# The first weight piece of a stage, loaded by the stage before it into a lasting tile, and small products placed behind two groups of the projections

## The reference, cut to what matters

```python
# first block, layer 0 (RWKV mixer, then a gated feed-forward), layer 1 (gated delta rule, feed-forward)
lerp = lambda i: u + xx * mu[i]
w_log = -softplus(-(w0 + tanh(lerp(3) @ w1) @ w2)) - 0.5      # w1: D x 64, w2: 64 x D
a = sigmoid(a0 + (lerp(4) @ a1) @ a2)                          # a1: D x 64, a2: 64 x D
...
proj = u @ w_in                                                # gated delta rule: D x (4 D + 16)
...
x = layer_norm(ALPHA * x + (1 + ga1) * (y @ w_out), ...)       # every mixer ends like this
gate, up = split(u @ ffn_w_in[i], 2)                           # D x 2*2816
x = layer_norm(ALPHA * x + (1 + ga2) * ((silu(gate) * up) @ ffn_w_out[i]), ...)
# second block: a state-space mixer (x @ w_in, D x 5152), mixture of experts, dilated attention, experts
```

## Time and profile before

| what | value |
|---|---|
| median of 3 runs | 4761.02 us (4743.81 to 4763.74) |
| the profiled execution's own time | 4764.29 us |
| its span, first to last instruction | 4762.6 us |
| PE busy | 3911.8 us, 82% of the span |
| VectorE, ScalarE, GpSimd busy | 34%, 15%, 15% |
| mean granted clock of PE | 0.904 of full speed |
| largest waits of PE | experts for their weights 127.8 us in 48, experts for VectorE 67.1 us in 66 |

### The profile page before, as it was taken

The page is one execution under the profiler, slowest core; times in us unless marked ns, Lnnn a source line. Parts: engine busy times, 40 slices in busy tenths (PEclk is TensorE's granted clock), DMA queues, the critical chain, the costliest instruction groups (busy, mean ns, idle before and its releaser), DMA issues. The chain is left out here.

```text
span 4762.6 us, 56977 instructions
## 1 busy us (share of the span) xinstructions
PE 3911.8 (82%) x23207; PEld 2625.4 (55%) x23207; DVE 1642.3 (34%) x3018; ACT 706.3 (15%) x1502; POOL 719.7 (15%) x595
## 2 busy tenths in 40 slices
PE   4989978999898878999899895877749977577773
PEld 2578855784446756864458743444427755344442
DVE  6667735530365653211341512000031143300003
ACT  2211211010222222100211500000010122000000
POOL 1123303330110213420100101000010033100001
PEclk9999978999899988999899896998969977699987
DMA  3221313623121012221221026999932100599995
GB/s 124 64 80 53 111 49 133 212 98 110 39 68 36 2 50 80 84 89 53 67 77 36 1 80 244 392 396 397 393 127 71 53 1 27 232 396 397 399 396 225
DMA packets 242989, 707.37 MB, mean 149 GB/s; under 512 B 22140, under 2 KB 117828, under 8 KB 192100
## 3 DMA queue, kind: packets, MB, share of 16 engines
q1 hardware_dynamic: 223060, 660.99, 37.5%
q10 hardware_dynamic: 15120, 26.76, 1.6%
q0 software_dynamic: 4608, 16.78, 0.9%
HBM read 667.24 MB, written 37.24 MB: 148 GB/s over the span
## 5 line engine op out<-in xcount | busy, mean ns | idle before, releaser
L3037 PE MATMUL experts_pg<-moe_wg,experts_xt 128*64 128x256 f32 x4224 | 529.4, 414 | 142.3 <-DMA moe_wg<-in_moe_w_up 127.8
L3037 PEld LDWEIGHTS experts_pg<-moe_wg,experts_xt 128*64 128x64 f32 x4224 | 334.5, 150 | 320.2 <-issue 178.0
L465 PE MATMUL ffn_out_y<-ffn_out_ring,ffn_h 128*128 128x512 f32 x704 | 308.8, 601 | 20.8 <-DMA ffn_out_ring<-in_ffn_w_out 20.8
L3052 PE MATMUL experts_py<-moe_wd,experts_ht 128*64 128x512 f32 x1056 | 256.4, 629 | 41.6 <-DVE experts_ht L3104 24.2
L86 PE MATMUL att_proj_ps<-att_proj_ring,ut 128*128 128x512 f32 x576 | 250.0, 597 | 15.6 <-DMA att_proj_ring<-in_attn_w_qkv 15.6
L3102 DVE TENSOR_TENSOR experts_h<-experts_hs,experts_pg 128x256 f32<-128x256 f32 x66 | 27.8, 421 | 659.2 <-ACT experts_hs L3071 659.2
L465 PEld LDWEIGHTS ffn_out_y<-ffn_out_ring,ffn_h 128*128 128x128 f32 x704 | 135.3, 193 | 190.5 <-issue 169.0
L562 PE MATMUL ffn_in_seven<-ffn_in_seven_t,ffn_in_seven_s 128*128 128x256 f32 x1056 | 238.4, 383 | 0.0
L86 PEld LDWEIGHTS att_proj_ps<-att_proj_ring,ut 128*128 128x128 f32 x576 | 177.5, 308 | 87.8 <-DMA att_proj_ring<-in_attn_w_qkv 16.0
L562 PEld LDWEIGHTS ffn_in_seven<-ffn_in_seven_t,ffn_in_seven_s 128*128 128x128 f32 x1056 | 204.0, 193 | 29.1
L562 PE MATMUL ffn_in_seven<-ut,ffn_in_ring 128*128 128x256 f32 x704 | 181.8, 404 | 19.1 <-DMA ffn_in_ring<-in_ffn_w_in 19.1
(11 more groups left out here) (651 smaller groups left out, 6294.0 us busy)
## 6 DMA issues: line engine op xcount, KB each, us to landing
moe_wg<-in_moe_w_gate SPq DMA_DIRECT2D x66, 2048.0 KB, 20.6
moe_wg<-in_moe_w_up SPq DMA_DIRECT2D x66, 2048.0 KB, 25.2
moe_wd<-in_moe_w_down SPq DMA_DIRECT2D x66, 2048.0 KB, 26.2
ffn_in_ring<-in_ffn_w_in SPq DMA_DIRECT2D x44, 1024.0 KB, 5.8
ffn_in_ada_ring<-in_ada_w SPq DMA_DIRECT2D x28, 1024.0 KB, 7.6
ffn_out_ring<-in_ffn_w_out SPq DMA_DIRECT2D x22, 1024.0 KB, 5.0
ssd_proj_ring<-in_ssd_w_in SPq DMA_DIRECT2D x20, 1024.0 KB, 5.3
att_proj_ring<-in_attn_w_qkv SPq DMA_DIRECT2D x9, 2048.0 KB, 7.9
```

Of the source, the lines that this page charges most:

```text
L465: last = nc.tensor.matmul(y[:, tt, half, :], h[:, kk, tt * P:(tt + 1) * P], ring[:, n % RING, q, half * BANK:(half + 1) * BANK], start=(kk ...
L3037: last = nc.tensor.matmul(pg[ch * SLOTS:(ch + 1) * SLOTS, b, side, 0:HH], xt[:, b, kk % MQ, kk // MQ, :], wg[:, b, side, kk, ch * HH:(ch + ...
L3052: last = nc.tensor.matmul(py[half * SLOTS:(half + 1) * SLOTS, b, :], ht[:, b, kk % HM, kk // HM, :], wd[:, b, kk, half * HALF:(half + 1) * ...
```

## The change

A tile `ahead` of 8 KB per partition and a semaphore live as long as the program does. Class `Ahead` holds a list of nine first pieces in the order of use; `next` issues the DMA of the next one. `Pieces` is a ring whose piece 0 is the lasting tile: its `load` issues nothing for piece 0, its `wait` for piece 0 is a wait on the lasting semaphore, and the pieces from 1 on use the slots of the ring in turn. `Ring` is the ring as it was.

```diff
+class Pieces:
+    def __init__(self, k, st, ring, shape):
+        self.ring, self.count, self.ahead, self.need = st.sb("ring", [P, ring] + shape), ring, k.ahead, k.ahead.total
...
+    def __getitem__(self, n):
+        return self.ring[:, (n - 1) % self.count] if n else self.first
+    def reused(self, n):
+        return n - self.count if n > self.count else None
+    def load(self, sp, n, src):
+        if n:
+            sp.dma_start(self[n], src).then_inc(self.loaded[(n - 1) % self.count], 16)
+    def wait(self, eng, n):
+        if n:
+            eng.wait_ge(self.loaded[(n - 1) % self.count], 16 * ((n - 1) // self.count + 1))
+        else:
+            eng.wait_ge(self.ahead.sem, self.need)
...
 start_stage, SP, behind the load of x:
+                for dst, part in low_rank:
+                    k.ahead.load(sp, dst, part)
...
 project_norm_stage(..., ahead=True, follow=False), ring of 4 as before:
-                    if n >= RING:
-                        sp.wait_ge(used, n - RING + 1)
-                    sp.dma_start(ring[:, n % RING, :, :], wv[:, n * PER:(n + 1) * PER, :]).then_inc(loaded[n % RING], 16)
+                    if ring.reused(n) is not None:
+                        sp.wait_ge(used, ring.reused(n) + 1)
+                    ring.load(sp, n, wv[:, n * PER:(n + 1) * PER, :])
+                if follow:
+                    if ahead:
+                        (sp.wait_ge(used, 1) if HEAD else sp.wait_ge(made, TT))
+                    k.ahead.next(sp)
...
 ffn_in, and at the end of SP's list:
-    CW, RING = 256, 4
+    CW, RING = 256, 3
+                    k.ahead.next(sp)
...
 gdn_proj (ssd_proj likewise, with its own names):
-            CW, RING, BANKS = 256, 3, 5
+            CW, RING, BANKS = 256, 2, 5
-                    pe.wait_ge(s["small_in"], 16)
-                    for tt in range(TT):
-                        last = accumulate(nc, pss[:, tt, :], [...])
-                    last.then_inc(s["small_made"], 1)
                     for g_ in range(GROUPS):
...
-                        if g_ == 2:
+                        if g_ == 1:
+                            pe.wait_ge(s["small_in"], 16)
+                            for tt in range(TT):
+                                last = accumulate(nc, pss[:, tt, :], [...])
+                            last.then_inc(s["small_made"], 1)
+                        if g_ == 3:
                             pe.wait_ge(s["g_done"], 1)
...
 rwkv_proj: the four DMAs of ScalarE are gone, w1, a1 and up are parts of the lasting tile
-                            pe.wait_ge(lora_in, 64)
+                            pe.wait_ge(k.ahead.sem, low_rank_in)
...
 rwkv_rec: gng and gnb are the two halves of the lasting tile
 att_proj: the ring lies in the memory of kqt; k.ahead.next(sp) at the end of SP's list
...
 program:
-    with ExitStack() as stack:
+    with Stage(nc, "kept") as kept, ExitStack() as stack:
```

More of the change, by code:

```diff
@@ L68, in __exit__, with __init__, load, next @@
         return False
+class Ahead:
+    def __init__(self, tile, sem, pieces):
+        self.tile, self.sem, self.pieces, self.total = tile, sem, pieces, 0
+    def load(self, sp, dst, src):
+        sp.dma_start(dst, src).then_inc(self.sem, 16)
+        self.total += 16
+    def next(self, sp):
+        src = self.pieces.pop(0)
+        self.load(sp, self.view(src.shape), src)
+    def view(self, shape):
+        return self.tile[:, 0:shape[1] * shape[2]].rearrange("p (a n) -> p a n", a=shape[1])
+class Pieces:
+    def __init__(self, k, st, ring, shape):
+        self.ring, self.count, self.ahead, self.need = st.sb("ring", [P, ring] + shape), ring, k.ahead, k.ahead.total
+        self.first = k.ahead.view([P] + shape)
+        self.loaded = [st.sem(f"loaded{i}") for i in range(ring)]
+    def __getitem__(self, n):
[10 more added lines that the diff above has]
+            eng.wait_ge(self.ahead.sem, self.need)
+class Ring(Pieces):
+    def __getitem__(self, n):
+        return self.ring[:, n % self.count]
+    def reused(self, n):
+        return n - self.count if n >= self.count else None
+    def load(self, sp, n, src):
+        sp.dma_start(self[n], src).then_inc(self.loaded[n % self.count], 16)
+    def wait(self, eng, n):
+        eng.wait_ge(self.loaded[n % self.count], 16 * (n // self.count + 1))
 class Chain:
@@ L433, in store, with project_norm_stage @@
         sp.wait_ge(self.stored, 16 * TT)
-def project_norm_stage(nc, k, name, h, n_k, w, ga_row, ln_g, ln_b, turn, out):
+def project_norm_stage(nc, k, name, h, n_k, w, ga_row, ln_g, ln_b, turn, out, ahead=True, follow=False):
     RING, PER = 4, 2
@@ L441, in project_norm_stage @@
     with Stage(nc, name) as st:
-        ring = st.sb("ring", [P, RING, PER, D])
+        ring = (Pieces if ahead else Ring)(k, st, RING, [PER, D])
         g, b = st.sb("g", [P, D]), st.sb("b", [P, D])
@@ L697, in _, with __init__ @@
                             nc.vector.tensor_tensor(h[:, 2 * c:2 * c + 2, :], act_out[:, :, :], both[:, 1, :, :], ALU.mult).then_inc(h_done, 1)
-        project_norm_stage(nc, k, f"ffn_out{l}", h, FK, w_out, ga_row, ln_g, ln_b, turn, out)
+        project_norm_stage(nc, k, f"ffn_out{l}", h, FK, w_out, ga_row, ln_g, ln_b, turn, out, follow=True)
 RWKV_HEADS, HD = 16, 64
+class LowRank:
+    def __init__(self, k):
+        pre = k.ahead.tile
+        self.w1, self.a1 = (pre[:, i * DK * HD:(i + 1) * DK * HD].rearrange("p (k n) -> p k n", k=DK) for i in range(2))
+        self.up = pre[:, 2 * DK * HD:2 * DK * HD + D]
 RWKV_GN_EPS = 64e-5
@@ L1504, in _ @@
                     gated(c)
-        project_norm_stage(nc, k, "rwkv_norm", bh, DK, p["w_out"], ga_row, ln_g, ln_b, turn, out)
+        project_norm_stage(nc, k, "rwkv_norm", bh, DK, p["w_out"], ga_row, ln_g, ln_b, turn, out, ahead=False, follow=True)
 class Softplus:
@@ L1608, in _ @@
                 def _(pe):
-                    pe.wait_ge(s["small_in"], 16)
-                    for tt in range(TT):
-                        last = accumulate(nc, pss[:, tt, :], [(k.ut[:, kk, 1 + tt * P:1 + (tt + 1) * P], small[:, kk, :]) for kk in range(DK)])
-                    last.then_inc(s["small_made"], 1)
                     for g_ in range(GROUPS):
@@ L2182, in _ @@
                     def _(pe):
-                        pe.wait_ge(s["small_in"], 16)
-                        for tt in range(TT):
-                            last = accumulate(nc, few[:, 0, tt, :], [(k.ut[:, kk, 1 + tt * P:1 + (tt + 1) * P], small[:, kk, :]) for kk in range(DK)])
-                        last.then_inc(s["small_made"], 1)
                         for g_ in range(GROUPS):
```

97 lines of the change are left out of this document (53 added, 44 removed).

## The result

The changed kernel takes 4721.41 us (median of 9 runs, 4704.99 to 4729.65); beside it the kernel before took 4757.91 (9 runs, 4742.48 to 4774.94). The ratio is 0.992, with a 95% interval of 0.9903 to 0.9938: 36.5 us less, where 50.5 had been predicted. Measured against the 4761.0 that the prediction started from, its 4710 was 11 us too low, and its range of 4688 to 4732 held the result. The distance would have been 3 us larger from the 4757.91 measured beside it. The profiled execution has an own time of 4727.83 us and a span of 4726.1 (before: 4764.3 and 4762.6).

The account below looks back on a forecast made before the run. The prediction took PE, busy 82% of the span, and its serial waits for first weight pieces as the bound. Terms 15.2 + 4.0 + 8.2 + 11.6 + 10.2 + 1.2 + 1.0 - 0.9 = 50.5 us gave 4710 us, range 4688 to 4732.

Parts of the forecast that it names:

- The wait and the clock of ffn_out: Both ffn_out starts: PE's first-piece wait shrinks, 15.2 us for the pair, and the clock does not fall, 4.0 us.
- ssd_norm: Start of ssd_norm: the wait from DMA issue to first product goes, 8.2 us; the clock is at 0.50 either way.
- gdn_norm: Start of gdn_norm: PE does piece 0 while waiting for piece 1, which takes that work out, 5.8 us.
- att_norm: Start of att_norm: piece 0's work, with its cold part, is done while waiting for piece 1, 5.8 us.
- The small products: gdn_proj and ssd_proj: 64 narrow products follow two groups later, take 8.6 us; gain 5.1 us each, 10.2 for both.
- The two cold starts: Projections: wide products begin at clock 0.50 at the stage's start and again behind the narrow ones, 2.4 us each.
- The case in which the clock holds: Rival: full clock through the narrow products, 9.3 us per projection in place of 5.1, 4702 us; chance 0.20.
- the one in which it falls at once: Rival: clock falls at every pause, narrow products gain nothing (-10.2), 31.5 us in all, 4729 us; chance 0.13.
- ffn_in: Start of both ffn_in: VectorE's token operations, taking turns with GpSimd's sums, delay the second product; gain 0.6 us each.
- The smaller ring, the added DMAs: Slots fall from 3 to 2 in projections, 4 to 3 in ffn_in; nine 1 MB DMAs added: no wait.
- The barrier's 0.9 us: Barrier of `kept`, from VectorE's end to the next DMA issue: a cost of 0.9 us.
- rwkv_proj: Low-rank weights' wait in rwkv_proj: LORA_A still needs all sixteen mixes; gain 1.0 us, between 2.0 and -0.5.

## Why the prediction was right, and where it was not

- **The wait and the clock of ffn_out** (19.2 predicted, 20.4 measured). Right in both steps. The clock at that start is not certain, though: in some executions of the variants one or both of the two stages started lower and took 1.7 us more (171.0 in place of 169.3, or 169.3 in place of 167.6), near the 2.0 that the prediction put on it. No run undoes this part alone; it rests on the rows and on stage lengths that repeat.
- **ssd_norm** (8.2, measured 7.2). Right in kind. Most of what is missing is the cold start: the clock rose 5.9 us behind the first product, before the change 4.3.
- **gdn_norm** (5.8, measured 4.9). Piece 1's products began 7.4 us after the start, close to the 7.6 of the earlier trace rows; the step that missed was that only one wait would come: piece 2 was late by 1.28 us too:

```profile
1739.44 3.70 PE L531 MATMUL gdn_norm_y<-gdn_norm_ring,gdn_kq 128*128 128x512 f32 x8 [1.49 <-DMA gdn_norm_ring<-in_gdn_w_out]
1744.42 7.13 PE L531 MATMUL gdn_norm_y<-gdn_norm_ring,gdn_kq 128*128 128x512 f32 x16 [1.28 <-DMA gdn_norm_ring<-in_gdn_w_out]
```

- **att_norm** (5.8, measured 1.3 to 3.4 in two profiles, 2.4 in the mean of all). The landing was foreseen (8.0 us after the start, against 7.9). The step that failed is "what goes is piece 0's work behind it, with its cold part". The clock was up at the start of the stage, so piece 0 took 3.67 us and not 5.8. It fell at the wait's end (0.4 us ahead of it in the second profile, 1.1 behind it in the first), so piece 1's products took 5.17 and 5.40 in place of about 3.6: the cold part moved behind the wait and stayed.
- **The small products** (5.1 each, measured 6.2 and 5.4). The assumption that narrow work counts for the clock like idling was right in kind: in gdn_proj the clock fell after 5 us of it, as assumed, and the 64 took 9.07 us against 8.6. In part that is luck: in ssd_proj, where the products have 32 columns, they took 8.38 us in both profiles but 11.05 in the run in which GpSimd waits, and that ssd_proj was only 1.6 us shorter than before. The two cold starts were cheaper than the 2.4 us each in the sum (15.76 and 15.46 us for 32 wide products in gdn_proj, against 13.91 at full clock). The case in which the clock holds is refuted by the windows (0.56), and so is the one in which it falls at once (1.00 for the first 4.5 us). By the rule of the Trainium skill that the clock follows how busy PE is ("TensorE: Matmul & The Clock Gate", the section cited before) the stretch of 8.9 busy us would have stayed at 1.00; the measured 0.56 decides against it, for 16-column products.
- **ffn_in** (0.6 each, measured 0.2 and -1.5). The contention and its turns were sized well: the second product came 9.0 us after the start, 8.5 predicted for the tokens, which leaves 0.1 to 0.2 us of the 0.6. What was left out is the clock in that wait, 1.7 us in the 24 products of ffn_in 1 (8.16 against 6.48) and 1.9 in ffn_in 0 (8.09 against 6.16), where a later wait gave most of it back.
- **The smaller ring, the added DMAs** (0): right, as the run with the rings alone shows for the first, and as the missing waits show for the second. The barrier's 0.9 us is not seen in the profiles.
- **rwkv_proj** (1.0, measured 0.4). LORA_A's 16 products ran at the lower clock for all of their 8.78 us, where 0.5 us had been put on it.
- **What no step had**: gdn_rec, 4.3 us longer through the clock. It is the largest single error; with the 5.8 us by which the stages above fell short of their 51.4 (and no 0.9 for the barrier) it makes 41 of the 50.5. The rest of the distance to the measured 36.5 is within its interval.

In short, the mechanisms held; the terms of att_norm and of the two ffn_in were short because a wait of about 4 to 5 us was priced at its own length alone, and gdn_rec gave back most of what gdn_proj had gained. Part of the error is hidden by terms that erred the other way (ffn_out, gdn_proj and ssd_proj, 2.6 us together).

## What to carry to other kernels

A first piece loaded ahead is worth its full wait only where it is large enough to cover the landing of the second; where it covers half, PE starts, waits, and can lose the full clock in that wait, so look at what it needs next (an operand of another engine, the second piece) and bring that forward too. Put small products between large ones and in short lots, and look at the clock behind the last lot. In a chain of short steps the granted clock decides the length, so count a gain only after looking at the stages behind it, and profile each kernel twice before believing a few us in a stage that nobody touched. A stage that repeats to 0.1 us can still move when a stage ahead of it changes its length.
